# State-space groups with both halves of y behind the last panel, norm rows from picking products, and a 32-column low-rank gate

## The chip, the cores and the metric

One core of one Trainium2 chip runs the whole program. The metric is the device time of one execution in microseconds (us), median of the runs; lower is better. All arrays are float32 in HBM. The engines are TensorE (PE), VectorE (DVE), ScalarE (ACT), GpSimd (POOL) and SyncE (SP, which here only issues loads and stores). Code lines are written L1942 and the like.

## What is computed

The reference is two transformer-like blocks on x of 256 tokens by 1024 columns. The parts that the change touches:

```python
def ssd_scan(...):   # 8 groups of 4 heads, state 128, chunks of 128 tokens
    cum = jnp.cumsum(a_c, axis=1)
    decay = jnp.exp(jnp.where(causal, seg, -jnp.inf))
    y_intra = jnp.einsum('bgij,bghij,bjghp->bighp', cb, decay, x_c)
    y_inter = jnp.einsum('bign,bghpn->bighp', C_c, state) * jnp.exp(cum)[..., None]

def gated_group_rms_norm(y, z, w, groups):
    g = y * silu(z)
    gs = g.reshape(*g.shape[:-1], groups, -1)
    gs = gs * lax.rsqrt(jnp.mean(jnp.square(gs), axis=-1, keepdims=True) + EPS)
    return gs.reshape(g.shape) * w

log_a = jax.nn.log_sigmoid(gate_lr @ w_gate_up[l] + b_gate[l]) / GLA_GATE_TAU   # gate_lr: 16 columns of xn @ w_in
```

## The kernel before, in words

Activations lie transposed (columns on the 128 partitions, 256 tokens free). Every large weight streams from HBM as panels of 128x1024 (512 KB) into four slots of `raw`. For each slot ACT makes a rounded high part (`split_hi`, L491, 128x1024, type fp32r), DVE the remainder (`split_lo`, L980), and PE multiplies hi by hi, hi by lo and lo by hi (`panel`, L1665 to L1667: 24 products of 256 columns per panel). The counters `landed`, `hi_done`, `taken` and `used` pass a slot from SP to ACT, DVE and PE; SP loads the next panel into a slot when DVE has taken the last one out.

Between the convolution and the output products lies the state-space stage: eight groups g, one call of `ssd` each on PE (L1898 on), `ssd_act` on ACT (L682 on), `ssd_dve` on DVE (L1215 on) and `ssd_side` on POOL (L399 on), written out for g = 0 and 7 and in a loop over pairs for 1 to 6. In each group PE works on four panels of z and the gates, `zg_panel(0)` to `zg_panel(3)`, and puts the scan's small products between them:

- after panel 0: transposes of x and B, C times B (`cb_mm`), and two sums of segments (`seg_mm`) from `a_upto_hi` (made by POOL, L406) and `a_upto_lo` (made by ACT in `upto_low`, L680, eight 128x128 operations);
- after panel 1: the cumulative sum, spread over the partitions (L1930, L1931, `cum_mm`), whose exponential ACT writes to `c_in` (L691) and POOL multiplies by C (L420);
- after panel 2: the last group's norm sums (L1891), the new state (L1938, `st_mm`), which ACT copies to `state` (L699), and y of the first chunk (L1942);
- after panel 3: y of the second chunk (L1948 from `decay`, L1949 from `c_in` and `state`), then DVE adds it up (L1237).

ACT's order inside a group is: copy `b_tok`, two exponentials to `decay`, the exponential to `c_in`, `upto_low` for the next group, the high parts of slots 0 and 1, the copy of the mean and of `state`, three copies to `stg`, the high parts of slots 2 and 3, the panel sum out of PSUM (L504), the silu of z (L660), and, when DVE has multiplied y by it (L1246, the gate product), a square (L666). DVE interleaves four panels of the modulation matrix, which use the same four slots of `raw` (L990, L992): so slot 1 holds first a modulation panel, which DVE must take out in the next `ssd_dve`, and then the z panel that ACT converts.

After group 7 comes the gated norm. ACT issues five small loads from its own queue (L717), takes the mean and the root; DVE inverts it and writes `g_diag`, four tiles of diagonal matrices (L1267); PE multiplies each by ones (L1973, 128x512, two behind panel 2 of the gm stage and two behind panel 3), which spreads the rows over all partitions; DVE scales y by them (L1274), ACT and DVE split the result (`yb_hi` L728, `yb_lo` L1280), and the next stage's first product needs the first quarter of that. Each engine runs its instructions in the order written; nothing reorders them.

In the second block the low-rank gate is three products for each of 8 tiles (L2046 to L2048, 16 columns of weights), scaled by DVE to `glr_sb` (L1390) and multiplied by `wgu` (L2057).

## Time and profile before

| what | value |
|---|---|
| median of 3 runs | 927.41 us (926.66 to 929.55) |
| span of the profiled execution, first to last instruction | 925.2 us |
| own time of the profiled execution | not listed apart; its span and the some 2.2 us that lie between span and median |
| PE busy | 915.6 us (99%) |
| DVE busy | 706.2 us (76%) |
| ACT busy | 565.7 us (61%) |
| POOL busy | 100.7 us (11%) |
| PE on the chain that ended last | 96% |
| mean granted TensorE clock | 0.997 |

The span is the time from the first to the last instruction. The page lists busy time of each engine, then the span in 40 slices, the queues, the chain of work that ended last, and the costliest groups of instructions. The timeline has one line for each run of equal instructions: start, length, engine, line, tiles and, in brackets, how long the engine had sat idle before it and what ended that. Products overlap in PE, so the length of one (0.28 us for 256 columns) is more than its share; the distance from one start to the next is what it costs.

### The profile page before, as it was taken

The page shows a single profiled execution, that of the slowest core. Times are in us where ns is not written, and L with a number is a line of the kernel's source. Part 1 is how long each engine was busy: PE and PEld are TensorE (multiplying, and loading weights), DVE is VectorE, ACT ScalarE, POOL GpSimd, SP SyncE. Part 2 cuts the span into 40 slices and gives each one's busy share as a digit, 9 for nine tenths or more (in the row PEclk, how much of TensorE's full clock was granted, in tenths as well). Part 3 has the DMA queues.
Part 4 walks back from the last instruction along what each step waited for, and adds up shares of the span by engine and source line. Part 5 has one row for each costly group of instructions (what it writes and reads, how often), then busy time and mean ns, then how long its engine had stood idle before and what let it go on. Part 6 is the DMA issues. An engine that isn't in the chain of part 4 may idle for free.

```text
span 925.2 us, 17436 instructions
## 1 busy us (share of the span) xinstructions
PE 915.6 (99%) x6700; PEld 845.9 (91%) x6700; DVE 706.2 (76%) x952; ACT 565.7 (61%) x827; POOL 100.7 (11%) x88
## 2 busy tenths in 40 slices
PE   9999999999999999999999999999999999999997
PEld 6799999999999989989888888999879999999886
DVE  5957888889988968568777556689886798877663
ACT  4376655687877765456555345566665776666453
POOL 0000300024423300010000001403100200000001
PEclk9999999999999999999999999999999999999999
DMA  9954455577767756545655655535423365655661
GB/s 355 361 177 156 163 193 182 180 234 258 228 232 250 245 175 209 183 147 174 201 186 188 194 186 183 162 134 183 136 92 117 116 200 186 202 182 183 195 210 48
DMA packets 85564, 175.53 MB, mean 190 GB/s; under 512 B 5424, under 2 KB 46912, under 8 KB 85504
## 3 DMA queue, kind: packets, MB, share of 16 engines
q1 hardware_dynamic: 84384, 172.12, 56.2%
q10 hardware_dynamic: 752, 1.27, 0.4%
q0 software_dynamic: 368, 1.31, 0.4%
q8 instruction: 41, 0.67, 0.3%
q14 instruction: 19, 0.16, 0.1%
HBM read 173.63 MB, written 1.05 MB: 189 GB/s over the span
## 4 chain that ended last, share of the span: by engine, by line
PE 96%; DVE 2%; ACT 1%; POOL 0%; issue 0%; DVEq 0%; POOLq 0%
PE proj_ps L1665 18%; PE proj_ps L1682 17%; PE proj_ps L1666 17%; PE proj_ps L1667 17%; PE proj_ps L1685 9%; PE proj_ps L1754 1%; PE aux L1795 1%; PE proj_ps L1755 1%; PE proj_ps L1756 1%; PE aux L1786 1%; PE aux L2084 1%; PE aux L2111 1%; PE aux L1948 1%; DVE mod_acc L992 1%; PE aux L1810 1%; PE aux L1942 1%
## 5 line engine op out<-in xcount | busy, mean ns | idle before, releaser
L980 DVE TENSOR_TENSOR w_lo<-raw,w_hi 128x1024 fp32r<-128x1024 f32 x276 | 343.2, 1256 | 125.7 <-ACT w_hi L491 125.2
L491 ACT CAST w_hi<-raw 128x1024 fp32r<-128x1024 f32 x276 | 286.1, 1047 | 171.0 <-PE proj_ps L1667 70.4
L1665 PE MATMUL proj_ps<-act_pair,w_hi 128*128 128x256 f32 x1016 | 289.9, 285 | 0.0
L1667 PE MATMUL proj_ps<-act_pair,w_lo 128*128 128x256 f32 x1016 | 287.3, 283 | 0.0
L1666 PE MATMUL proj_ps<-act_pair,w_hi 128*128 128x256 f32 x1016 | 287.3, 283 | 0.0
L1665 PEld LDWEIGHTS proj_ps<-act_pair,w_hi 128*128 128x128 f32 x1016 | 194.7, 192 | 3.7 <-issue 1.5
L1666 PEld LDWEIGHTS proj_ps<-act_pair,w_hi 128*128 128x128 f32 x1016 | 194.8, 192 | 0.6
L1667 PEld LDWEIGHTS proj_ps<-act_pair,w_lo 128*128 128x128 f32 x1016 | 194.7, 192 | 0.0
L1682 PE MATMUL proj_ps<-ff_pair,w_hi 128*128 128x512 f32 x256 | 69.9, 394 | 0.0
L1682 PE MATMUL proj_ps<-act_pair,w_hi 128*128 128x512 f32 x248 | 67.7, 394 | 0.0
L439 POOL TENSOR_TENSOR tmp_b<-tmp_b 128x512 f32<-128x512 f32 x4 | 5.2, 1294 | 458.4 <-ACT tmp_b L514 458.4
L1682 PE MATMUL proj_ps<-glu_pair,w_hi 128*128 128x512 f32 x176 | 50.0, 395 | 0.0
L1682 PEld LDWEIGHTS proj_ps<-ff_pair,w_hi 128*128 128x128 f32 x256 | 43.7, 189 | 5.9
L1682 PEld LDWEIGHTS proj_ps<-act_pair,w_hi 128*128 128x128 f32 x248 | 42.4, 189 | 5.7
L992 DVE SCALAR_TENSOR_TENSOR mod_acc<-raw,silu_c,mod_acc 128x1024 f32<-128x1024 f32 x28 | 45.4, 1623 | 1.2 <-DMA raw<-in_panels 0.9
L1685 PEld LDWEIGHTS proj_ps<-ff_pair,w_lo 128*128 128x128 f32 x256 | 39.3, 189 | 5.5
L1685 PEld LDWEIGHTS proj_ps<-act_pair,w_lo 128*128 128x128 f32 x248 | 38.1, 189 | 5.3
L1685 PE MATMUL proj_ps<-ff_pair,w_lo 128*128 128x256 f32 x256 | 40.7, 281 | 0.0
L1685 PE MATMUL proj_ps<-act_pair,w_lo 128*128 128x256 f32 x248 | 39.5, 281 | 0.0
L1195 DVE SCALAR_TENSOR_TENSOR conv_acc<-proj_ps,cols,conv_acc 128x255 f32<-128x255 f32 (+2 forms) x96 | 38.7, 471 | 0.0
L1665 PE MATMUL proj_ps<-yb_hi,w_hi 128*128 128x256 f32 x128 | 36.3, 284 | 0.2 <-issue 0.2
L1667 PE MATMUL proj_ps<-yb_hi,w_lo 128*128 128x256 f32 x128 | 36.2, 283 | 0.0
(355 smaller groups left out, 1639.0 us busy)
## 6 DMA issues: line engine op xcount, KB each, us to landing
raw<-in_panels SPq DMA_DIRECT2D x308, 512.0 KB, 3.6
mod_first<-in_panels SPq DMA_DIRECT2D x16, 512.0 KB, 10.3
xres<-in_x_t SPq DMA_DIRECT2D x2, 512.0 KB, 5.5
wst<-in_ws_t POOLq DMA_DIRECT2D x1, 512.0 KB, 3.8
bs_sb<-in_bs_rows POOLq DMA_DIRECT2D x1, 512.0 KB, 4.6
level_sb<-in_levels ACTq DMA_DIRECT2D x1, 512.0 KB, 5.4
out_t<-tmp_a SPq DMA_DIRECT2D x1, 512.0 KB, 2.6
out_t<-tmp_a SPq DMA_DIRECT2D x1, 384.0 KB, 3.0
```

The lines of the kernel that those rows point to most:

```text
L491: nc.scalar.copy(w_hi[:, s, :], raw[:, s, :]).then_inc(hi_done, 1)
L980: tt(out=w_lo[:, s, :], in0=raw[:, s, :], in1=w_hi[:, s, :].bitcast(F32), op=ALU.subtract).then_inc(taken, 1)
L992: stt(out=mod_acc[:], in0=src, scalar=c_k, in1=mod_acc[:], op0=ALU.mult, op1=ALU.add).then_inc(done, 1)
L1195: ins = stt(out=out, in0=behind_nt, scalar=w(NT * c + nt, taps - 1 - back), in1=out, op0=ALU.mult, op1=ALU.add)
L1665: mm(dst, hi, xh, start=first and k == 0 and nt % 2 == 0, stop=False, skip_group_check=True)
L1666: mm(dst, hi, xl, start=False, stop=False, skip_group_check=True)
L1667: ins = mm(dst, lo, xh, start=False, stop=last and k == ks - 1, skip_group_check=True)
L1682: mm(bank, w_hi[:, s, n:n + P], flat(x_pair[:, k_at]), start=first and k == 0, stop=False, skip_group_check=True)
L1685: ins = mm(bank[:, T:2 * T], w_lo[:, s, n:n + P], x_hi[:, k_at], start=False, stop=False, skip_group_check=True)
L1754: mm(dst, xh, wh, start=first and k == 0, stop=False)
L1755: mm(dst, xh, wl, start=False, stop=False)
L1756: ins = mm(dst, xl, wh, start=False, stop=last and k == 1)
```

## The change

Four edits, which touch three stages.

1. **State-space group, PE.** `zg_panel(2)` goes ahead of the cumulative sum, so that this sum stands behind the third panel; y of the first chunk goes behind panel 3, directly ahead of y of the second chunk, and its wait asks for both decay tiles.
2. **State-space group, ACT.** The high part of slot 0 goes ahead of the exponential to `c_in`, the one of slot 1 behind it, and `upto_low` behind both, so that it stands directly ahead of the copies of the mean and of `state`.
3. **Gated norm.** `g_diag` is gone. DVE writes the inverse roots as a high part (columns 0 to 7) and a remainder (columns 32 to 39) of `g_part`; two products with a rounded identity turn them into rows (behind panel 1), ACT copies these to `g_rows`, and eight products with weights that pick one row and its remainder spread them over the partitions (behind panel 2). POOL makes `g_part`'s zeros, the identity and the picking weights behind its last group.
4. **Low-rank gate.** The high part and remainder of the weights stand side by side in 32 columns, so two products for each of 8 tiles take the place of three; rows 16 to 31 of the result are the remainder's, and `wgu` is loaded twice, into 32 partitions, so that the next product adds them. ACT's queue issues six loads in place of five.

```diff
@@ ssd_side, behind the last group
+            pool.wait_ge(S["cum_mm"], SSD_GROUPS + 1)
+            nc.gpsimd.memset(g_part[:].bitcast(F32), 0.0).then_inc(S["made_ok"], 1)
+            nc.gpsimd.tensor_tensor(out=ident_r[:], in0=ident, in1=ident, op=ALU.mult).then_inc(S["made_ok"], 1)
+            nc.gpsimd.tensor_tensor(out=pick_r[:], in0=ident[:, 0:SSD_GROUPS], in1=ident[:, 32:32 + SSD_GROUPS], op=ALU.add
+                                    ).then_inc(S["made_ok"], 1)
@@ ssd_act
+                split_hi(nxt, 0, landed_nxt)
                 act.wait_ge(S["cum_mm"], g + 2)
                 nc.scalar.activation(flat(c_in[:]), aux[:, 0], ACT.Exp).then_inc(S["ecum_ok"], 1)
+                split_hi(nxt, 1, landed_nxt)
                 if not last:
                     upto_low(g + 1)
-                split_hi(nxt, 0, landed_nxt)
-                split_hi(nxt, 1, landed_nxt)
                 act.wait_ge(S["st_mm"], g + 1)
                 if not first:
                     group_mean(g - 1)
@@ ACT, gated norm
-            for dst, src in ((rope_sb, rope_d), (level_sb, levels_d), (neg_sb, neg_d), (wgu, wgu_d), (wglr, wglr_d)):
-                act.dma_start(dst[:], src).then_inc(S["late_in"], 16)
+            for dst, src in ((rope_sb[:], rope_d), (level_sb[:], levels_d), (neg_sb[:], neg_d), (wgu[0:16, :], wgu_d), (wgu[16:32, :], wgu_d),
+                             (wglr[:], wglr_d)):
+                act.dma_start(dst, src).then_inc(S["late_in"], 16)
...
             split_hi(GROUP["ssm"], 0)
+            act.wait_ge(S["grow_mm"], 1)
+            nc.scalar.copy(g_rows[:], aux[:, 1, 0:T]).then_inc(S["copies_ok"], 1)
             split_hi(GROUP["ssm"], 1)
@@ DVE, gated norm
-            for q in range(4):
-                tt(out=g_diag[:, q], in0=spread(ident, 1, 4), in1=spread(g_stat[:, 1, 2 * q:2 * q + 2].rearrange("p g t -> p (g t)"), 2, P),
-                   op=ALU.mult).then_inc(S["gdiag_ok"], 1)
+            dve.wait_ge(S["made_ok"], 1)
+            roots = g_stat[:, 1].rearrange("p g t -> p t g")
+            g_hi, g_lo = g_part[:, :, 0:SSD_GROUPS], g_part[:, :, 32:32 + SSD_GROUPS]
+            step(nc.vector.tensor_copy(g_hi, roots))
+            tt(out=g_lo, in0=roots, in1=g_hi.bitcast(F32), op=ALU.subtract).then_inc(S["gpart_ok"], 1)
@@ ssd
                 zg_panel(1)
+                zg_panel(2)
                 pe.wait_ge(S["xdt_ok"], g + 1)
                 mm(aux[:, 0], ones_r[:], flat(a_upto_hi[:, 1]), start=True, stop=False)
                 mm(aux[:, 0], ones_r[:], flat(a_upto_lo[:, 1]), start=False, stop=True).then_inc(S["cum_mm"], 1)
-                zg_panel(2)
...
-                pe.wait_ge(S["m_ok"], g * 2 + 1)
+                zg_panel(3)
+                pe.wait_ge(S["m_ok"], g * 2 + 2)
                 for h in range(HPG):
                     mm(y(h, 0), xdt[:, 0, 64 * h:64 * h + 64], decay[:, 0, h], start=True, stop=True)
-                zg_panel(3)
-                pe.wait_ge(S["m_ok"], g * 2 + 2)
                 pe.wait_ge(S["state_ok"], g + 2)
                 pe.wait_ge(S["cin_ok"], g + 1)
@@ PE, gm stage
-                for q in ((), (), (0, 1), (2, 3))[s]:
-                    pe.wait_ge(S["gdiag_ok"], q + 1)
-
-                    pe.wait_ge(*((S["ecum_ok"], 9), (S["gs_ok"], 9), (S["y_ok"], 10), (S["mod_done"], 6))[q])
-                    mm(aux[:, q], ones[:], flat(g_diag[:, q]), start=True, stop=True).then_inc(S["grow_mm"], 1)
+                if s == 1:
+                    pe.wait_ge(S["made_ok"], 3)
+                    pe.wait_ge(S["gpart_ok"], 1)
+                    pe.wait_ge(S["gs_ok"], 9)
+                    for t in range(TT):
+                        ins = mm(aux[:, 1, t * P:t * P + P], g_part[:, t], ident_r[:], start=t == 0, stop=True, skip_group_check=True)
+                    ins.then_inc(S["grow_mm"], 1)
+                if s == 2:
+                    pe.wait_ge(S["copies_ok"], 2)
+                    for g in range(SSD_GROUPS):
...
+                        ins = mm(aux[:, q, (g % 2) * T:(g % 2) * T + T], spread(pick_r[:, g], 1, P), g_rows[:], start=g % 2 == 0,
+                                 stop=True, skip_group_check=True)
@@ PE, low-rank gate
-                dst = aux[0:16, 0, 0:T]
-                mm(dst, wglr_hi[:, k], pre2_hi[:, k], start=k == 0, stop=False)
-                mm(dst, wglr_hi[:, k], pre2_lo[:, k], start=False, stop=False)
-                ins = mm(dst, wglr_lo[:, k], pre2_hi[:, k], start=False, stop=k == KT - 1)
+                dst = aux[0:32, 0, 0:T]
+                mm(dst, flat(wglr_pair[:, k]), pre2_hi[:, k], start=k == 0, stop=False)
+                ins = mm(dst, flat(wglr_pair[:, k]), pre2_lo[:, k], start=False, stop=k == KT - 1)
```

The order of ACT's instructions in a state-space group, here group 0 from its exponentials to `decay` on; groups 1 to 6 repeat it. In these rows `w_hi<-raw` is the high part of a slot, slot 0 first. Before:

```order
L687 ACTIVATE decay<-aux 128x512 x2
L691 ACTIVATE c_in<-aux 128x512
L680 ACTIVATE a_upto_lo<-square,a_lo 128x128 x8
L491 CAST w_hi<-raw 128x1024 x2
L699 COPY state<-aux 128x256
L641 COPY stg<-xbc 128x512
```

With the change (the lines are those of the changed kernel):

```order
L695 ACTIVATE decay<-aux 128x512 x2
L499 CAST w_hi<-raw 128x1024
L700 ACTIVATE c_in<-aux 128x512
L499 CAST w_hi<-raw 128x1024
L688 ACTIVATE a_upto_lo<-square,a_lo 128x128 x8
L707 COPY state<-aux 128x256
L649 COPY stg<-xbc 128x512
```

The eight operations on `a_upto_lo` stood ahead of both conversions and now stand between the second one and the copy of `state`.

ACT at the gated norm, from the last of its small loads to the first copy of `yb_hi`. Before:

```order
L717 DMA wglr<-in_wglr 128x128
L671 COPY g_stat<-aux 128x2
L721 ACT_TABLE_LOAD
L721 ACTIVATE g_stat<-g_stat,eps 128x16
L722 ACT_TABLE_LOAD
L722 ACTIVATE zg<-zg 128x2048
L491 CAST w_hi<-raw 128x1024 x2
L725 ACTIVATE zg<-zg 128x2048
L728 CAST yb_hi<-xbc 128x1024
```

With the change:

```order
L726 DMA wgu<-in_wgu 16x256 x2
L726 DMA wglr<-in_wglr 128x128
L679 COPY g_stat<-aux 128x2
L730 ACT_TABLE_LOAD
L730 ACTIVATE g_stat<-g_stat,eps 128x16
L731 ACT_TABLE_LOAD
L731 ACTIVATE zg<-zg 128x2048
L499 CAST w_hi<-raw 128x1024
L734 CAST g_rows<-aux 128x256
L499 CAST w_hi<-raw 128x1024
L736 ACTIVATE zg<-zg 128x2048
L739 CAST yb_hi<-xbc 128x1024
```

One load more is issued ahead of the mean, and the copy to `g_rows`, with its wait for PE's two turning products, stands between the two conversions.

## Rows read from the trace of the kernel before

**Rows 1.** The page, part 1 (busy us, share of the span, instructions)

```profile
PE 915.6 (99%) x6700; PEld 845.9 (91%) x6700; DVE 706.2 (76%) x952; ACT 565.7 (61%) x827; POOL 100.7 (11%) x88
```

**Rows 2.** Waits of PE: who waited for whom, us in total, times, longest us

```profile
PE aux L1795 <- DVE zero L1091: 2.1, 1, 2.1
```

**Rows 3.** Timeline of PE, group 3: start us, us, instruction

```profile
250.57 0.39 PE L1665 MATMUL proj_ps<-act_pair,w_hi 128*128 128x256 f32 x1
...
253.63 0.45 PE L1948 MATMUL aux<-decay,xdt 128*64 128x128 f32 x4
```

**Rows 4.** Timeline of ACT, group 3

```profile
246.35 0.60 ACT L691 ACTIVATE c_in<-aux 128x512 f32<-128x512 f32 x1 [0.83 <-PE aux L1931]
246.84 2.44 ACT L680 ACTIVATE a_upto_lo<-square,a_lo 128x128 fp32r<-128x128 f32 x8
...
250.89 1.05 ACT L491 CAST w_hi<-raw 128x1024 fp32r<-128x1024 f32 x1 [0.68 <-DMA raw<-in_panels]
...
251.90 0.38 ACT L699 COPY state<-aux 128x256 f32<-128x256 f32 x1
...
254.95 1.05 ACT L491 CAST w_hi<-raw 128x1024 fp32r<-128x1024 f32 x1 [0.60 <-DMA raw<-in_panels]
```

**Rows 5.** Timeline of DVE, its gate product of groups 2 and 3

```profile
241.50 0.69 DVE L1246 TENSOR_TENSOR xbc<-xbc,zg  x1 [0.17 <-ACT zg L660]
...
259.06 0.69 DVE L1246 TENSOR_TENSOR xbc<-xbc,zg  x1 [0.94 <-ACT zg L660]
```

**Rows 6.** Timeline of SP: the load of slot 1, and all loads (the page, part 6)

```profile
246.53 0.34 SPq L297 DMA_DIRECT2D raw<-in_panels  x1
...
raw<-in_panels SPq DMA_DIRECT2D x308, 512.0 KB, 3.6
```

**Rows 7.** Timeline of PE, the same instruction two groups apart

```profile
241.80 0.48 PE L1926 MATMUL aux<-a_upto_hi,after_r 128*128 128x512 f32 x1
...
277.12 0.48 PE L1926 MATMUL aux<-a_upto_hi,after_r 128*128 128x512 f32 x1
```

**Rows 8.** Timeline of PE, norm rows and what follows

```profile
336.79 1.88 PE L1973 MATMUL aux<-g_diag,ones 128*128 128x512 f32 x4
...
343.45 0.36 PE L1665 MATMUL proj_ps<-yb_hi,w_hi 128*128 128x256 f32 x1 [0.18 <-issue]
```

**Rows 9.** Timeline of ACT at the gated norm

```profile
330.72 0.45 ACTq L717 DMA_DIRECT2D wgu<-in_wgu  x1
...
332.04 0.16 ACT L671 COPY g_stat<-aux 128x2 f32<-128x2 f32 x1 [2.06 <-PE aux L1891]
...
341.04 1.05 ACT L728 CAST yb_hi<-xbc 128x1024 fp32r<-128x1024 f32 x1 [0.29 <-DVE xbc L1274]
```

**Rows 10.** Timeline of DVE at the gated norm

```profile
333.93 0.25 DVE L1265 RECIPROCAL g_stat<-g_stat 128x16 f32<-128x16 f32 x1 [3.54 <-ACT g_stat L721]
334.21 2.50 DVE L1267 TENSOR_TENSOR g_diag<-square,g_stat 128x512 f32<-128x512 f32 x4
...
342.12 1.22 DVE L1280 TENSOR_TENSOR yb_lo<-xbc,yb_hi 128x1024 fp32r<-128x1024 f32 x1 [1.11 <-ACT yb_hi L728]
```

**Rows 11.** Timeline of ACT: a copy of 128x256 from PSUM in another stage

```profile
605.65 0.37 ACT L526 COPY rr_sb<-aux 128x256 f32<-128x256 f32 x1 [1.24 <-PE aux L1779]
```

**Rows 12.** Timeline of PE, DVE and POOL: low-rank gate product, first level

```profile
609.76 0.28 PE L2046 MATMUL aux<-pre_hi,wglr_hi 128*16 128x256 f32 x1
...
612.49 0.28 PE L1665 MATMUL proj_ps<-act_pair,w_hi 128*128 128x256 f32 x1
...
613.92 0.41 DVE L1390 TENSOR_TENSOR glr_sb<-aux,rr_sb 16x256 f32<-16x256 f32 x1
...
635.72 0.87 POOL L473 TENSOR_TENSOR gx<-gqk,gd 128x256 f32<-128x256 f32 x1
...
636.97 1.16 PE L2084 MATMUL aux<-gx 64*128 64x128 f32 x16
```

**Rows 13.** Windows of 2 us: busy (x), then PEclk (granted clock), DMA share, GB/s

```profile
22.00:24.00 2.00, 2.00 (x3) 0.82 (x3) 1.79 (x6) 0.91 (x2) 0.72 (x1) 0.50 1.05 400
```

More of the change, by code:

```diff
@@ L139, in two_blocks @@
         yb_lo = at("yb_lo", 88, [16, T], F32R)
-        g_diag = at("g_diag", 152, [4, 4, P])
+        g_part = at("g_part", 160, [TT, P], F32R)
+        g_rows = at("g_rows", 161, [T], F32R)
+        pick_r = at("pick_r", 162, [SSD_GROUPS], F32R)
+        ident_r = at("ident_r", 162.5, [P], F32R)
         g_sq = at("g_sq", 202.5, [2, T])
@@ L250, in two_blocks @@
             "an engine's own steps": "dve_step pool_step",
-            "memsets and first conversions": "ready c_ready narrow_hi_ok narrow_ok ws_masked",
+            "memsets and first conversions": "ready c_ready narrow_hi_ok narrow_ok copies_ok ws_masked made_ok",
             "modulation": "mod_acc_ok mod_mm mod_done",
@@ L258, in two_blocks @@
                    "btok_ok decay_ok ecum_ok state_ok",
[L259 removed]
+            "gated group norm": "silu_z sig_ok g_ok g2_ok gsq_ok gs_mm gs_ok grt_ok gpart_ok grow_mm yb_f yb_h yb_ok",
             "mixers' sum": "mix_f mix_h mix_ok",
             "first MLP": "sq_ok ffhi_ok ff_ok",
[L262 removed]
+            "GLA": "glr_mm glr_ok gate_mm gx_abs gx_exp gx_u gx_ln gx_inv lev_d lev_e lev_x lev_mm lev_ok "
                    "og_mm og_sq og_ms og_rt og_diag og_row gla_f gla_h gla_ok",
@@ L634, in _ @@
             nc.scalar.copy(after_r[:], after)
-            nc.scalar.copy(ones_r[:], ones[:]).then_inc(S["sums_ok"], 1)
+            nc.scalar.copy(ones_r[:], ones[:]).then_inc(S["copies_ok"], 1)
             def group_tiles(g, par):
@@ L779, in _ @@
             scale2 = lambda k: small[:, 88 + k:89 + k]
-            act.wait_ge(S["late_in"], 80)
-            nc.scalar.copy(wglr_hi[:], wglr[:]).then_inc(S["narrow_hi_ok"], 1)
+            act.wait_ge(S["late_in"], 96)
+            nc.scalar.copy(wglr_hi, wglr[:]).then_inc(S["narrow_hi_ok"], 1)
             unscaled_hi(range(4), pre2_hi, RES_FF2, scale2)
```

33 lines of the change are left out of this document (18 added, 15 removed).

## The prediction

> **What bounds the kernel now.** I read the page's busy times first: PE is busy 99% of the span [rows 1]. Then the waits of PE: the longest is 2.1 us ahead of its very first product [rows 2], and no wait of PE in the state-space stage is in the list at all. So PE's own instructions set the end, and the change can act in two ways: take products away from PE, or make PE wait where it does not now. The first is counted from distances between starts; for the second the timelines of ACT, DVE and SP beside PE must be read, since the change reorders ACT and leaves PE's slack to be found out. The chip's differences of under about 0.3% (2.8 us) can't be told from no change here.
>
> **Low-rank gate (edit 4).** The 24 products run from 609.76 to 612.49, 0.114 us each [rows 12]. Eight go: 0.9 us less for PE. The next reader of the result, DVE's scaling, ends at 614.33 on a chain of its own and PE would come about then, so that wait stays near zero. But the first level product that needs POOL starts at 636.97, and POOL's operand was complete at 636.59 [rows 12]: 0.4 us of slack. If that chain doesn't move with PE, only 0.4 us of the 0.9 stays. Bounds 0 and -0.9; I take **-0.4**, since the slack row is the nearest thing to a limit.
>
> **Gated norm (edit 3).** PE's side: two pairs of diagonal products, 1.88 us each pair [rows 8], so 3.8 us go; ten short products at the 0.114 us of [rows 12] come, 1.1 us. PE alone would gain 2.6 us. But the stage behind starts at 343.45, just after DVE's first `yb_lo` ends at 342.12 + 1.22 = 343.34 [rows 8, 10]: that chain sets the start, not PE. Its links are ACT's. It was late already: the mean was copied 2.06 us after ACT fell idle of computing, because ACT's queue was issuing loads [rows 9]. One more load costs the 0.45 us of its neighbour [rows 9]. The copy to `g_rows` costs the 0.37 us of an equal copy [rows 11]. Against both stands ACT's idle 0.29 us ahead of `yb_hi` [rows 9]. Sum 0.45 + 0.37 - 0.29 = 0.53. DVE's side loses four `g_diag` products, 2.50 us, for two tiny ones (the reciprocal of 128x16 is the nearest, 0.25 each) [rows 10]; that moves only work that waits for ACT afterwards. PE also waits twice inside: its turning products need `g_part` at about 334.18 + 0.45 + 0.5 = 335.1, while panel 1 ends some 2.9 us (24 products at 0.12) ahead of the 336.79 of [rows 8], at 333.9: 1.2 us. It would catch up none of this by the saving, as the chain ends it anyway. So the 2.6 us are not gained, and the net is **+0.6**; bounds -2.6 (chain hidden after all) and +1.5 (the 0.29 us not there, ACT later). POOL's three setup operations stand behind its last group's work; POOL is busy 11% [rows 1], and I count nothing. If that cover fails, each costs PE at most what a POOL operation here takes, 0.9 us [rows 12].
>
> **State-space groups, PE (edit 1).** The same products in another place. Between panel 3's first product and y's second chunk lie 253.63 - 250.57 = 3.06 us [rows 3]. What a change of neighbour does to a start is about 0.1 to 0.2 us either way (3.06 against 24 times 0.12 = 2.88), so eight groups are bounded by -1.6 and +1.6; I take 0. The exponential to `c_in` moves a panel later, from 246.35 [rows 4] to about 249.2; POOL's product behind it is then done by about 251.9, if it takes at most twice the 0.87 us of its other operations [rows 12] and a start; y needs it from 253.6 on. Covered by panel 3. What is queued behind ACT's longer wait is the conversion of slot 1, whose panel lands only at 250.8 anyway.
>
> **State-space groups, ACT (edit 2): the term that decides.** In group 3 the conversion of slot 1 starts at 250.89, ended by the landing of its panel, and `state` is copied from 251.90 to 252.28 [rows 4]. PE needs `state` for y at 253.63 [rows 3]. Slack: 1.35 us. Before, the eight `a_upto_lo` operations, 2.34 us from start to next start (246.84 to 249.18), ran while ACT had nothing to convert [rows 4]. Now they run behind the slot 1 conversion, and nothing but the landing decides when that is. So `state` is ready at 252.28 + 2.34 = 254.62: PE waits **1.0 us**. That is the first turn.
>
> It doesn't stop there, because ACT, DVE and SP form a ring. From the slot 1 conversion ACT goes on to the `stg` copies, slots 2 and 3, the panel sum and the silu; then DVE's gate product, its modulation panels 0 and 1; then SP's load into slot 1, and the next conversion. ACT's part, 250.89 to 259.06, is 8.17 us, of which 0.60 was a wait for slot 3's landing [rows 4, 5]; with the 2.34 us inside and the 0.60 swallowed it is 9.91. DVE's and SP's part, 241.50 to 250.89, is 9.39 [rows 4, 5]. The ring becomes 19.3 us. PE's group takes (277.12 - 241.80) / 2 = 17.66 us [rows 7]. So the ring would be 1.6 us longer than PE's group and becomes the bound: first turn 1.0, then five more groups up to group 6 (group 7 makes no next `a_upto_lo`), 1.0 + 5 x 1.64 = 9.2 us. That is the upper bound. Downwards: slot 1's load takes 250.89 - 246.53 = 4.36 us, behind its neighbours, while the median of all loads is 3.6 [rows 6]. With loads further apart it would tend to that, 0.76 less a turn: 1.0 + 5 x 0.88 = 5.4 us. The lowest end is the first turn alone, 1.0, if the ring has slack that I don't see. I take **6.0**, near the lower of the two rings, since a late ACT spaces SP's loads by itself. At the end ACT is late against PE by part of a turn, and the gated norm's chain starts from there: bounds 0 and +1.0, I take +0.3.
>
> The Trainium skill, page "DMA: Bandwidth & Descriptors", section "Anatomy of one DMA — SWDGE (gpsimd) path", gives a DMA (one issued from GpSimd; these come from SP) some 2.0 us fixed and its bytes at 436 GB/s, an estimate of 3.2 us for 512 KB. By that the ring would be 18.1 us, and this term 1.0 + 5 x 0.5 = 3.5 instead of 6.0, the time 931.4. The trace disagrees for this slot, with 4.36 us.
>
> **Sum**, against the profiled execution: 925.2 - 0.4 + 0.6 + 0 + 6.0 + 0.3 = 931.7 us of span. Around the span lie 2.2 us (927.41 - 925.2, the profiled execution taken as a median one), so **933.9 us**, +0.7%.
>
> **Rivals.**
>
> *A, the ring stays open: no change.* The first turn's 1.0 us is paid once, then PE's own delay gives ACT its slack back. For it: ACT was idle 0.68 and 0.60 us ahead of two of its conversions [rows 4], so some of what is inserted fills idle time, and the ring is read from one group alone. Against it: 19.3 against 17.66 us. Time: 927.4 + 1.0 + 0.6 - 0.4 = 928.6.
>
> *B, PE's saved products count: faster.* The place is the copy of `state` in each group: if it lies 1.0 us earlier than I work out (slot 1 landing at 249.8 instead of 250.8), PE does not wait, and if the gated norm's chain is also shorter, since DVE loses 2 us of `g_diag`, PE gains its 2.6. Time: 927.4 - 2.6 - 0.9 - 0.8 (half of the bound of edit 1) = 923.1. It decides from a landing under 3.4 us after issue on. For it: PE is at 99%, and every product removed was on its path. Against it: ACT's idle row names the DMA.
>
> *C, the clock falls as well.* The granted clock was 0.50 from 22 to 24 us, in a stretch with thin products, and PE was busy all of it [rows 13]: such a drop costs 1 us for each 2 us that it lasts. Waits of 1 to 2 us in each group could bring it about. Six drops: 933.9 + 6 = 940. Against it: nothing shows that a wait of 1 us does this. The Trainium skill, page "TensorE: Matmul & The Clock Gate", section "A second HAM failure mode: psum-queue depth-cycling", tells of a kernel whose short idle times between groups of products made the clock go up and down; by it this rival would be the forecast. No row here shows it.
>
> *D, the change doesn't do what it says.* The conversions could run ahead of landings they wait for in another count. The order of ACT's instructions shows the move, so I give this nothing of its own.
>
> **Chances and range.** My forecast (the ring closes, 930.5 to 938) 0.66; A 0.17; B 0.12; C 0.05. Slower by over 0.3% (above 930.2) takes the forecast and C, less a little of the forecast's low end, plus the top of A: 0.70. Within 0.3%: 0.18. Faster: 0.12. The range reaches down into A and up over the ring's likely sizes: 926.5 to 938. The forecast's own range is 930.5 to 938.
>
> **What would show it.** Right: PE lists waits for ACT's `state` copy, under 0.5 us in some groups and 1 to 2.5 in others, together 5 to 9; the distance of two groups grows from 35.3 to 37 or more; ACT's conversion of slot 1 is still ended by a DMA and `a_upto_lo` follows it; PE waits about 1.2 us for `g_part`; the stage behind the norm starts 6 us or more later. Wrong: no wait of PE in the groups and the distance still 35.3, or the first product on `yb_hi` earlier than 343.4. If the clock is under 0.99 in the groups, C holds.

## The result, and the profile after

The changed kernel is slower: 939.39 us (median of 4 runs, 937.4 to 942.8) against 927.95 for the kernel before, a ratio of 1.0127 with a 95% interval of 1.0106 to 1.0148. Run again beside other kernels it took 939.65 (median of 6 runs, 934.0 to 947.8). The direction, the place and the largest term of the forecast were right. The time lies 5.5 us above the forecast and 1.4 us above its range.

The profiled execution (the one of 937.4 us, the fastest of the four) spans 935.7 us, 10.5 more than before. Its page, part 1:

```profile
PE 917.6 (98%) x6694; PEld 850.8 (91%) x6694; DVE 699.3 (75%) x950; ACT 565.0 (60%) x828; POOL 102.3 (11%) x91
```

PE has six products fewer than in [rows 1] and is busy 2.0 us longer. Idle time alone could not do that: some products take longer. The waits of PE (us in total, times, longest us) now begin with a line that [rows 2] did not have:

```profile
PE aux L1960 <- ACT state L707: 6.8, 5, 2.4
PE aux L1808 <- DVE zero L1102: 2.1, 1, 2.1
PE proj_ps L1678 <- issue: 1.0, 1, 1.0
```

The timeline of ACT in group 3 answers to [rows 4]:

```profile
250.73 1.05 ACT L499 CAST w_hi<-raw 128x1024 fp32r<-128x1024 f32 x1 [1.61 <-DMA raw<-in_panels]
251.69 0.59 ACT L700 ACTIVATE c_in<-aux 128x512 f32<-128x512 f32 x1
253.70 1.05 ACT L499 CAST w_hi<-raw 128x1024 fp32r<-128x1024 f32 x1 [1.42 <-DMA raw<-in_panels]
254.65 2.44 ACT L688 ACTIVATE a_upto_lo<-square,a_lo 128x128 fp32r<-128x128 f32 x8
...
257.04 0.36 ACT L707 COPY state<-aux 128x256 f32<-128x256 f32 x1
```

And PE at the same place, with [rows 3] to compare:

```profile
255.10 0.66 PE L1956 MATMUL aux<-decay,xdt 128*64 128x128 f32 x8
257.46 0.45 PE L1960 MATMUL aux<-decay,xdt 128*64 128x128 f32 x4 [1.70 <-ACT state L707]
```

`upto_low` stands behind a conversion whose start waited for a landing, and the copy of `state` behind `upto_low`; PE sits idle for 1.70 us. Over all groups the waits are 1.17, 1.30, 0.22, 1.70, 0, 2.41, 0, 0: uneven, as when PE runs up to a slower chain. Two groups take 36.7 to 40.5 us instead of the 35.32 of [rows 7].

The rest is the clock. Windows of the changed kernel (busy, then PEclk, DMA share, GB/s):

```profile
294.00:295.00 1.00, 0.05 (x2) 0.06 (x3) 1.00 (x1) 1.00 (x5) 0.68 (x1) 1.00 0.05 8
296.00:302.00 6.00, 6.00 (x30) 5.80 (x28) 3.84 (x5) 4.86 (x7) 0.00 (x0) 0.50 0.69 221
303.00:304.00 1.00, 1.00 (x12) 1.00 (x12) 0.00 (x0) 0.00 (x0) 0.31 (x1) 1.00 0.59 225
340.00:343.00 3.00, 3.00 (x16) 3.00 (x17) 0.00 (x0) 1.20 (x2) 0.00 (x0) 0.52 0.98 367
927.00:930.00 3.00, 3.00 (x11) 1.97 (x11) 0.17 (x1) 0.66 (x2) 0.00 (x0) 0.54 0.00 0
```

PE was idle up to 294.95, its longest wait; from 295.8 to 302.6 the granted clock stands at half (1.2 instead of 2.4 GHz), and PE does 30 products in 6 us (some of them longer ones) where it does 12 in one us just behind. What this costs is read from the same stretch of products with and without the drop, from y's second chunk to the next group's segment sums, in groups 5 and 3:

```profile
294.95 0.45 PE L1960 MATMUL aux<-decay,xdt 128*64 128x128 f32 x4 [2.41 <-ACT state L707]
...
304.69 0.47 PE L1939 MATMUL aux<-a_upto_hi,after_r 128*128 128x512 f32 x1
```

```profile
264.15 0.48 PE L1939 MATMUL aux<-a_upto_hi,after_r 128*128 128x512 f32 x1
```

It takes 9.74 us with the drop and 264.15 - 257.46 = 6.69 without: 3.0 us. The clock also stands at half at 340, behind a wait of 0.65 us for the last square, and at 927, at the end of the program.

Where the 10.5 us lie is told by how far the same product is behind its place in the trace of before:

| product | before | changed | behind by |
|---|---|---|---|
| last run of products of y, group 7 | 324.99 | 333.53 | 8.54 |
| first product on `yb_hi` | 343.45 | 353.19 | 9.74 |
| first gate product | 609.76 | 619.48 | 9.72 |
| second level product | 636.97 | 646.15 | 9.18 |
| end of the span | 925.2 | 935.7 | 10.5 |

- The groups cost 8.5 us: 6.8 of waits for `state` and 3.0 of clock, less 1.3 for the PE order's shorter groups and other small differences.
- The norm stage costs 1.2 us, none of it the clock's. Between the copy of the panel mean and the first product on `yb_hi` lie 11.4 us in both kernels (332.04 to 343.45 and 341.78 to 353.19). The mean is copied 1.2 us later behind the last y: 0.8 because ACT's last square comes later (5.16 us behind that y instead of 4.36), and 0.4 because ACT's queue then issues six loads. The drop at 340 falls into time that PE has to spare before `yb_hi`, where it is idle for 1.04 us even so.
- The gate gives back 0.5 us. Its own products are 0.9 us shorter, as the lines below show, but the level products behind it wait for POOL: 26.67 us lie between the first gate product and the second level product, where [rows 12] have 27.21.
- The drop at 927 costs 1.3 us. It stands in code that the change does not touch, some 600 us behind the last wait in the groups; the second profile of the changed kernel (`after_again`, below) has none there while PE works, so nothing shows that the change brought it about.

```profile
619.48 0.28 PE L2070 MATMUL aux<-pre_hi,wglr_pair 128*32 128x256 f32 x1
...
621.30 0.28 PE L1678 MATMUL proj_ps<-act_pair,w_hi 128*128 128x256 f32 x1
...
646.15 1.16 PE L2107 MATMUL aux<-gx 64*128 64x128 f32 x16
```

That is 1.82 us between the first two starts, where [rows 12] have 2.73.

### The profile page after: what moved, and what is told of

It is laid out like the page before. It is cut to its first block, busy times and chain, and to the rows that moved or that the text cites. A ratio compares the mean times of both kernels' runs of the same rounds, so it can differ in the third digit from the quotient of the medians.

```text
span 935.7 us, 17426 instructions
## 1 busy us (share of the span) xinstructions
PE 917.6 (98%) x6694; PEld 850.8 (91%) x6694; DVE 699.3 (75%) x950; ACT 565.0 (60%) x828; POOL 102.3 (11%) x91
## 4 chain that ended last, share of the span: by engine, by line
PE 79%; DVE 6%; ACT 6%; DMA 4%; issue 3%; POOL 1%; ACTq 0%; DVEq 0%; SPq 0%; POOLq 0%
PE proj_ps L1695 17%; PE proj_ps L1678 14%; PE proj_ps L1679 13%; PE proj_ps L1680 13%; PE proj_ps L1698 9%; DMA raw<-in_panels 3%; DVE mod_acc L1003 2%; PE proj_ps L1767 1%; DVE w_lo L991 1%; PE proj_ps L1768 1%; PE proj_ps L1769 1%; ACT a_upto_lo L688 1%; ACT w_hi L499 1%; PE aux L1799 1%; DMA mod_first<-in_panels 1%
## 5 line engine op out<-in xcount | busy, mean ns | idle before, releaser
L991 DVE TENSOR_TENSOR w_lo<-raw,w_hi 128x1024 fp32r<-128x1024 f32 x276 | 348.9, 1276 | 126.4 <-ACT w_hi L499 125.6
L1003 DVE SCALAR_TENSOR_TENSOR mod_acc<-raw,silu_c,mod_acc 128x1024 f32<-128x1024 f32 x28 | 39.2, 1399 | 1.0 <-DMA raw<-in_panels 0.7
```

The costliest lines, as they stand in the source:

```text
L991: tt(out=w_lo[:, s, :], in0=raw[:, s, :], in1=w_hi[:, s, :].bitcast(F32), op=ALU.subtract).then_inc(taken, 1)
L1003: stt(out=mod_acc[:], in0=src, scalar=c_k, in1=mod_acc[:], op0=ALU.mult, op1=ALU.add).then_inc(done, 1)
```

## Experiments

Three theories. **R**: what stands on ACT between the cumulative sum and `state`, or the ring of ACT, DVE and loads, makes PE wait. **C**: the granted clock falls behind such waits and costs extra. **P**: PE's own length, or its new order, counts. Later ones are split off: L (a local chain on ACT ahead of the `state` copy), D (DVE's product into `decay` has no slack left) and N (ACT's queue of small loads sets the norm's chain). All ratios are to the kernel before, run on the same chip beside them (926.98 to 927.51 us).

### The two orders apart

`low_first`, against the changed kernel:

```diff
                 nc.scalar.activation(flat(c_in[:]), aux[:, 0], ACT.Exp).then_inc(S["ecum_ok"], 1)
-                split_hi(nxt, 1, landed_nxt)
                 if not last:
                     upto_low(g + 1)
+                split_hi(nxt, 1, landed_nxt)
```

> The changed kernel with one line moved on ACT: the conversion of slot 1 of the next panel stands behind the eight upto_low instead of ahead of them; all else as in the change. Theory R (the waits come from ACT's order: the eight upto_low, 19.5 us a turn against PE's 17.6): the waits of PE before y's second chunk (6.8 us in all in the changed kernel) are gone, two groups take 35.2 us again, and the time falls by 6.8 us at least, to about 932. Theory C (the drops of the granted clock at 295.8 and 340.1 come behind those waits, and cost about 4 us): they are gone too, and the time is near 926, a little below the kernel before, as the gate's 0.9 us and the PE order's 0.7 us are left. Theory P (the waits come from PE's own new order, which needs m and xdt earlier or later): the waits and the 939 stay.

Measured: 931.02 us, 1.0044 (1.0027 to 1.0062). One line on ACT takes back some 8 of the 11.4 us. The waits fell from 6.8 to 2.7 us and no clock drop is left in the groups. But 926 was not reached; something else costs.

`act_order_only` is the kernel before with edit 2 alone, `pe_order_only` the kernel before with edit 1 alone (the diff of the change, those lines only).

> The kernel before with the ACT order alone (slots 0 and 1 of the next panel converted ahead of the eight upto_low). Theory R: PE waits for the second product's state copy as in the changed kernel, 5 to 8 us over eight groups, and the time is 933 to 936. With theory C the clock falls behind the largest of these waits, 2 to 4 us more: 936 to 939. Theory P: no wait, 927.4.

Measured: 936.34 us, 1.0101 (1.0064 to 1.0138); 5.5 us of waits at that place, and a clock of 0.5 for 3.4 us behind one of 1.3 us. As R and C say. (The profile names no releaser for these waits; the place is y's second chunk, which waits for `state`.)

> The kernel before with the PE order alone (y's first chunk behind the group's last panel, the spread cumulative sum behind the third). Theory R: no new wait; the products saved (0.09 us a group in the changed kernel) give 0.7 us: 926.7. Theory P: PE waits before y or the spread sum, and the time is 932 to 939.

Measured: 933.35 us, 1.0063 (1.0042 to 1.0084). A miss for what I had written under R; the time is in the range written under P, a new order that makes PE wait. PE waits for `state` in seven groups:

```profile
PE aux L1947 <- ACT state L699: 6.5, 7, 1.3
```

each 0.87 to 0.89 us but the first, with no growth: not a ring, but a local chain. ACT and PE in group 3 of that kernel:

```profile
251.90 0.60 ACT L691 ACTIVATE c_in<-aux 128x512 f32<-128x512 f32 x1 [2.33 <-PE aux L1932]
252.39 2.44 ACT L680 ACTIVATE a_upto_lo<-square,a_lo 128x128 fp32r<-128x128 f32 x8
254.73 1.98 ACT L491 CAST w_hi<-raw 128x1024 fp32r<-128x1024 f32 x2
...
256.67 0.37 ACT L699 COPY state<-aux 128x256 f32<-128x256 f32 x1
```

```profile
257.09 0.45 PE L1947 MATMUL aux<-decay,xdt 128*64 128x128 f32 x4 [0.87 <-ACT state L699]
```

The cumulative sum comes a panel later, ACT stands still for 2.33 us waiting for it, and the 5.1 us of work from `c_in` to `state` don't fit before y.

Neither order is harmless: one costs 6.4 us alone and the other 9.4, and the whole change 11.4 to 12.1. So the two do not add up. That each uses up the same slack, the 1.35 us that I had found between `state` and y, would explain it; no run shows it apart.

### Which half of the PE order

`cum_move_only` moves the cumulative sum alone (L1930, L1931 behind `zg_panel(2)`), `y_move_only` y's first chunk alone (L1942 behind `zg_panel(3)`), both in the kernel before.

> The kernel before with the spread cumulative sum alone moved behind the third panel. Theory L: the whole of what the PE order costs is here. The sum comes 2.9 us later, of which 1.35 us were slack and 0.68 us idle: PE waits 0.9 us in each of seven groups, 933 to 934. If it is the move of y's first chunk instead: 927.

> The kernel before with y's first chunk alone moved behind the last panel. Theory L: nothing waits, since y's second chunk starts where it did, and the products between two kinds saved give 0.09 us a group: 926.3. If the first chunk's move costs PE's order its slack: 930 or more.

Measured: 934.10 us, 1.0069 (1.005 to 1.0088), and 928.56 us, 1.0005 (0.9984 to 1.0026). The sum's move carries the loss, with 0.74 to 0.75 us of wait in each of six groups after a first one of 1.14. The other move can't be told from no change. Its waits are of another kind:

```profile
PE aux L1943 <- DVE decay L1232: 2.5, 3, 1.2
```

The first chunk used to need only the first half of DVE's product into `decay`; behind the last panel PE asks for both halves 0.66 us (the length of the first chunk) sooner than before.

### Other orders on ACT and DVE

`state_first` and `state_then_slot`, against the changed kernel (the second has `split_hi(nxt, 1, ...)` ahead of `upto_low`, otherwise the same):

```diff
                 nc.scalar.activation(flat(c_in[:]), aux[:, 0], ACT.Exp).then_inc(S["ecum_ok"], 1)
-                split_hi(nxt, 1, landed_nxt)
-                if not last:
-                    upto_low(g + 1)
                 act.wait_ge(S["st_mm"], g + 1)
                 if not first:
                     group_mean(g - 1)
                 nc.scalar.copy(state[:], aux[:, 1, 0:T]).then_inc(S["state_ok"], 1)
+                if not last:
+                    upto_low(g + 1)
+                split_hi(nxt, 1, landed_nxt)
```

> The changed kernel with ACT's copies of the panel mean and of state right behind the exponential to c_in, then the eight upto_low, then the conversion of slot 1. Theory L (a local chain: what stands on ACT between the spread cumulative sum and the state copy makes PE wait, 0.9 us a group in the PE order alone, whose waits did not grow from group to group): no wait of PE ahead of y's second chunk, two groups take 35.2 us, no drop of the granted clock in the groups, the time is 925 to 926.5. Theory R (the ring of ACT, DVE and SP is longer than PE's group whatever its order): the wait turns up elsewhere, at a panel or at the transposes, 4 to 6 us in all, time 930 to 934.

> As the one before, but the conversion of slot 1 ahead of the eight upto_low, as in the change. Theory L: as before it, 925 to 926.5. Theory R: the ring has the 2.4 us of upto_low inside again (between the conversions of slot 1 and slot 3), so that PE waits at the panels of the next group, 5 us or more, and the time is 932 or more.

Measured: 932.52 us, 1.0051 (1.0033 to 1.007), and 934.65 us, 1.0083 (1.0062 to 1.0104). Theory L falls, R holds: no line for `state` is left, but two groups still take 35.7 to 36.8 and 36.7 to 37.9 us. The wait turned up at DVE's product into `decay` (2.6 us in both), at the modulation columns (0.9 and 3.7 us) and, in group 7, at POOL's product behind `c_in` (0.9 us in both).

`state_first_dve` is `state_first` with DVE's fourth modulation panel of a group moved behind both products into `decay`; `y_late_dve` has that edit, y's first chunk late, and otherwise both old orders (with the norm and gate edits).

```diff
+                mod_panel_of(2)
                 for c in range(2):
-                    mod_panel_of(2 + c)
                     dve.wait_ge(S["decay_ok"], g * 2 + (c + 1))
...
                        op=ALU.mult).then_inc(S["m_ok"], 1)
+                mod_panel_of(3)
```

> The kernel with the state copy first (on record above: 932.5 us; PE waited 2.6 us for DVE's product into decay, 0.9 for POOL's product behind c_in, 0.9 for a modulation column) with DVE's fourth modulation panel behind the second product into decay. Theory D: the 2.6 us go, the others may stay: 929 to 931. If the ring of loads behind it sets the pace whatever the order: 932 to 934, the wait at another place.

> The changed kernel with ACT's old order and the cumulative sum back behind the second panel, so that of the two orders only y's first chunk behind the last panel is left; and on DVE the fourth modulation panel of a group moved behind the second product into decay. Theory D (with y's first chunk late PE needs that second product 0.7 us earlier, and DVE, 0.8 us ahead of it in group 3 before, has no slack left): now DVE has 2 us more, PE does not wait, two groups take 35.15 us, and the time is 926.0 - 0.7 = 925.3. If the waits stay (DVE's lateness comes from the gate product before, not from its own order): 927 to 929.

Measured: 932.52 us, 1.0058 (1.0039 to 1.0078), and 935.72 us, 1.0085 (1.0065 to 1.0104). The first is where `state_first` was. The second is the clearest miss of the study: 7 us slower than `y_move_only`, which is y's late chunk without the DVE edit (and without the norm and gate edits, which change nothing that can be told, as shown below). The waits for `decay` are gone, as theory D had it, and others, larger, stand in their place:

```profile
PE aux L1940 <- DVE modc L1027: 6.0, 3, 2.7
PE aux L1944 <- DVE xdt L1232: 2.5, 4, 0.8
```

Why is seen on ACT, at the conversion of slot 3 in group 3:

```profile
261.38 1.05 ACT L499 CAST w_hi<-raw 128x1024 fp32r<-128x1024 f32 x1 [2.35 <-DMA raw<-in_panels]
```

The modulation panel sits in slot 3 of `raw` until DVE has taken it; taken later, it lets the next load start later, and the 0.60 us of wait for that landing in [rows 4] has become 2.35. ACT's panel sum and silu come later by that, then DVE's gate product, then everything DVE does for the next group. This is the ring, closed through a load.

### The clock: filling PE's idle time

`fill`, against the changed kernel, puts six products a group between y's first chunk and the wait for `state`; `fill_more` has twelve of them. They write to a part of PSUM that the next panel overwrites. `after_again` is the changed kernel once more.

```diff
+                for n in range(0 if last else 6):
+                    mm(proj_ps[:, par, 0:256], after_r[:], x_hi[:, n], start=True, stop=True)
                 pe.wait_ge(S["state_ok"], g + 2)
```

> The changed kernel with six products more on PE (128x256, 0.12 us each, 0.7 us in all) in groups 0 to 6, ahead of its wait for the state copy; their result is overwritten, so nothing of the output changes. Theory R (another chain sets the pace and PE only waits for it): the waits shrink by what is filled, the places of y stay, and the products cost nothing, except in the groups without a wait (0.7 us each, three of seven): 937 to 941. If the clock's drops came from the idle time as such, they go with it, and the time is 1 to 3 us lower than that: 935 to 938. If PE's own length counts (theory P): 939.4 + 7 x 0.7 = 944.

> The changed kernel with twelve filler products (1.4 us) in groups 0 to 6 ahead of PE's wait for the state copy. Theory R and C (the pace is another chain's, and PE's idle time lets the granted clock drop): waits under 1.5 us in all, no or one drop in the groups, and a time of 936 to 940, though PE has 9.8 us more of products than the changed kernel. Theory P (PE's own length counts in full): 939.4 + 9.8 = 949.

> The changed kernel once more, beside the kernels with filler products, on one chip. 937 to 942, mean granted clock 0.983 to 0.992, as in its first four runs; a profile with 5 to 8 us of waits for the state copy, and at least one stretch at a clock of 0.5 between 200 and 350 us.

Measured:

| kernel | added to PE (7 groups) | median us | ratio (95%) | mean granted clock over its runs | waits for `state`, profiled run |
|---|---|---|---|---|---|
| changed kernel, again | none | 939.65 | 1.0133 (1.0089 to 1.0177) | 0.989 | 6.7 us |
| fill | 5.4 us | 935.87 | 1.0095 (1.0070 to 1.0121) | 0.993 | 2.4 us |
| fill_more | 10.9 us | 937.44 | 1.0107 (1.0079 to 1.0136) | 0.997 | none |

(The added time is 84 products at the 0.13 us that each takes, by the two-group distance below; for the 42 of `fill` it is an estimate from that.) With 10.9 us of useless work PE is no slower: P as PE's own length, by which `fill_more` would take 949 us, is out, and another chain sets the pace. That `fill` is faster is likely and not beyond doubt, since its interval and those of the two sets of the changed kernel (1.0106 to 1.0148 and 1.0089 to 1.0177) overlap a little. It is what R and C together give: the work fits into time in which PE would have waited, so it costs little, and PE falls idle less, so the clock stays. The clock in the groups says the same: the two profiles of the changed kernel have one drop and three there, `fill` and `fill_more` none. The unfilled kernel, run beside `fill_more`:

```profile
259.66 0.45 PE L1960 MATMUL aux<-decay,xdt 128*64 128x128 f32 x4 [2.28 <-ACT state L707]
```

```profile
262.00:269.00 7.00, 7.00 (x42) 7.00 (x42) 3.32 (x5) 4.08 (x5) 0.73 (x1) 0.63 0.72 215
```

and, with twelve fillers, its clock over the whole span:

```profile
core 0: 935.3 us, clock 1.000
```

The 1.000 owes something to luck: this execution also lacks the drop near the program's start that the other profiles have, in a stretch that no kernel here changes. With twelve the groups are evenly 38.25 us a pair, the 35.15 of PE's own products (the 36.91 of `pe_order_only` less its two waits of 0.88) and two fillings of 1.55: there PE itself sets the pace again. Six are nearer to what the other chain leaves free.

How much is clock in all? In the profiled execution it is 4.3 of the 10.5 us, 3.0 in the groups and 1.3 at the end. Over all runs only an upper figure can be had. The span times the mean granted clock is what a run would take at the full clock throughout, roughly. Its median is 922.3 us over 83 runs of the kernel before, and 926.4 and 927.8 us over the two sets of the changed kernel. So of the 11.4 to 12.1 us of loss 4 to 5.5 us remain at the full clock, and at most some 7 us are clock; at most, because a drop in time that PE has to spare, as at 340, is counted here and costs nothing.

The Trainium skill, page "TensorE: Matmul & The Clock Gate", section "A second HAM failure mode: psum-queue depth-cycling", describes this kind of case: short idle times between groups of products that make the clock go down and up. The traces agree, with 6.8 us at half clock behind a wait of 2.4 us. They also show that idle time is not enough by itself: `pe_order_only` waited 0.88 us in every group and kept a mean clock of 0.996, as the kernel before, and `y_late_dve` waited 2.73 us ahead of the segment sums of a group, with a full panel right behind, and had no drop there. And it is not needed everywhere: in `y_move_only` the clock fell from 332.2 to 335.8, in the norm stage, though PE had not waited as much as 0.2 us in the 40 us before; what stood there were sixteen products of one column each and a full panel:

```profile
329.99 0.95 PE L1786 MATMUL aux<-ones,mod_acc 128*128 128x1 f32 x8
331.08 1.05 PE L1891 MATMUL aux<-avg_g,g_sq 128*128 128x1 f32 x8
332.00 0.36 PE L1665 MATMUL proj_ps<-ya_hi,w_hi 128*128 128x256 f32 x1
```

### Norm and gate edits

`norm_rows_only` is the kernel before with edit 3 alone; `norm_gate` has edits 3 and 4 with both old orders.

> The kernel before with the norm edit alone (transpose by four products, copy on ACT, eight picking products). In the changed kernel this stretch lost 1.2 us, with a clock of 0.5 for 3.4 us at 340. If that drop belongs to the waits of the groups ahead of it: no drop here, the first product on yb_hi 0.5 us sooner to 0.3 us later than before, the time 927 to 928. If the drop belongs to the norm's own short wait and short products: the clock falls at 331 to 335 here too, and the time is 928.5 to 929.5.

> The changed kernel with both engines' orders in the state-space groups put back (edits 1 and 2 undone), norm and gate edits kept. No wait of PE in the groups, two groups take 35.33 us, no drop of the granted clock between 26 and 920 us. The norm edit alone gave 0.34 us in the trace, the gate's eight products 0.9 us: span 925.2 - 0.3 - 0.9 = 924.0, time about 926.0, faster than both kernels by a little. If the norm or the gate edit had a share in the changed kernel's loss: 928 or more.

Measured: 927.26 us, 0.9998 (0.9978 to 1.0019), and 928.07 us, 1.0006 (0.9988 to 1.0023). Neither can be told from the kernel before. The traces say more than the times do. The first product on `yb_hi`, at 343.45 before [rows 8], starts at 343.12 with the norm edit, and at 344.23 with the gate edit on top, though that edit touches nothing of the norm but ACT's list of loads. From the copy of the mean to that product it is 11.4 us in all three, so the norm edit takes nothing off the chain and adds nothing to it; the 0.33 us come from ACT's queue, whose last load took 0.72 us to issue in the trace of before and 0.44 in `norm_rows_only`. The timeline of ACT in `norm_gate`, to be read beside [rows 9]:

```profile
330.67 1.52 ACTq L726 DMA_DIRECT2D wgu<-in_wgu  x2
332.22 0.48 ACTq L726 DMA_DIRECT2D wglr<-in_wglr  x1
332.83 0.16 ACT L679 COPY g_stat<-aux 128x2 f32<-128x2 f32 x1 [2.89 <-issue]
```

The two loads of `wgu`, of 16x256 each, take 1.52 us to issue, where the one took 0.45, and the panel mean is copied at 332.83, against 332.04 before and 331.71 with the norm edit alone. So the 0.5 us that the gate edit saves behind 610 us, and more, are lost at 331 us, on a queue that nobody would look at for a low-rank gate.

So the loads were moved behind the conversions of `yb` (`late_only`: in the kernel before, with its five loads; `norm_gate_late`: with edits 3 and 4, whose diff against the changed kernel is shown without its old orders):

```diff
-            for dst, src in ((rope_sb[:], rope_d), (level_sb[:], levels_d), (neg_sb[:], neg_d), (wgu[0:16, :], wgu_d), (wgu[16:32, :], wgu_d),
-                             (wglr[:], wglr_d)):
-                act.dma_start(dst, src).then_inc(S["late_in"], 16)
             group_mean(7)
...
+            for dst, src in ((rope_sb[:], rope_d), (level_sb[:], levels_d), (neg_sb[:], neg_d), (wgu[0:16, :], wgu_d), (wgu[16:32, :], wgu_d),
+                             (wglr[:], wglr_d)):
+                act.dma_start(dst, src).then_inc(S["late_in"], 16)
             for j in range(2):
```

> The kernel before with ACT's five loads for the level stage moved from ahead of the last panel mean to behind the conversions of yb. Theory N (ACT's queue, busy with issuing loads for 2.1 us, sets the gated norm's chain, and so the start of the stage behind): ACT copies the mean 1.7 us sooner, and the first product on yb_hi comes up to 1.0 us sooner; PE's own products (two diagonal pairs, 3.8 us) then bound it. 926.0 to 927.0. If PE's products set it: no change, 927.3.

> Norm and gate edits with both old orders, and the six loads moved behind the conversions of yb. With the loads ahead (on record: norm and gate edits) the sixth load cost the norm's chain 1.1 us and gave the gate's 0.9 back. Theory N: the mean is copied 2.5 us sooner, PE has 2.6 us less of products, and the first product on yb_hi comes 1.5 to 2.5 us sooner than in that kernel: span 923.0 to 924.0, time 924.8 to 925.8, the fastest of all. If ACT's two sigmoids and conversions set it anyway: 926.5 or more.

Measured: 927.44 us, 0.999 (0.9972 to 1.0008), and 927.02 us, 0.999 (0.9973 to 1.0007). The chain of `norm_gate_late` is shorter:

```profile
331.14 0.16 ACT L679 COPY g_stat<-aux 128x2 f32<-128x2 f32 x1 [1.21 <-PE aux L1904]
```

```profile
342.54 0.35 PE L1678 MATMUL proj_ps<-yb_hi,w_hi 128*128 128x256 f32 x1 [1.05 <-issue]
```

1.7 us sooner than in `norm_gate`. The profiled span is 923.7 us, the shortest of all kernels here; by its interval the time is not shown to be faster than before. With the loads moved in the kernel before alone, the stretch from the last y to the first product on `yb_hi` is 0.8 us shorter (325.90 to 343.59, against 324.99 to 343.45). In that trace one more wait of PE takes it back, 1.0 us for DVE's product into `decay` in group 1, ahead of any edited place. Why the median shows no gain either, no run here tells.

## Why the prediction was wrong in size

- **What bounds, and where it would show: right.** PE waits for ACT's `state` copy, five waits with 6.8 us in all; the forecast was 6.0, and "together 5 to 9". The two-group distance is over 36.7. The value lies between the two rings that I worked out (5.4 and 9.2).
- **The step that failed: the sum counted the clock at nothing.** It stood as rival C with 0.05, "against it: nothing shows that a wait of 1 us does this". The term is 4.3 us in the profiled execution (3.0 behind the wait of 2.41 us, 1.3 at the end of the program) and at most some 7 us over the runs. C's sign, a clock under 0.99 in the groups, came true: it is 0.98 from 190 to 334 us, in the row below this item. C's figure, 940, is close to what was measured (939.4), in part by luck: it had six drops of 2 us, one a group, and there were one of 6.8 us in one profile and three of 3.4 to 6.8 us in the other. The chance given was too small, and the range should have reached to C, since its condition (waits of 1 to 2 us, from my own sum) was met by the forecast itself: C was no rival to the ring but its consequence, though not a sure one.

```profile
190.00:334.00 144.00, 137.19 (x1142) 130.43 (x1140) 117.21 (x118) 106.47 (x191) 50.07 (x40) 0.98 0.70 226
```

- **The rest of the distance is small.** The forecast has 931.7 us of span, the profile 935.7. The waits are 0.8 us more than the 6.0, the clock 4.3, the norm stage 1.2 instead of 0.9; the groups are otherwise 1.3 shorter than the 0 of edit 1, and the gate gives 0.1 more. The other 2.0 us of the median are that the profiled execution was the fastest of four; the two slowest, of 940.60 and 942.78 us, had a lower mean clock (0.987 and 0.983 against its 0.990).
- **Edit 1 "takes 0": wrong as a statement on the edit.** I worked out the late cumulative sum with ACT's new order only. Alone it costs 6.4 us (933.35 against 926.98). On top of edit 2 it can't be told from nothing (1.0101 with edit 2 alone, 1.0127 with all four, and the intervals overlap). PE's own products are 0.09 us a group shorter in `pe_order_only`, inside the bounds of 1.6.
- **Edit 2: right in size (6.8 us of waits against 6.0), with too simple a cause.** With `upto_low` back ahead of slot 1 (`low_first`) the kernel is still 4 us slower than before, since a part of edit 1's loss then shows. The 1.35 us of slack that I read was the slack of one chain. DVE's product into `decay` had another, which I did not read at all. In the trace of before, group 3:

```profile
251.55 1.25 DVE L1232 TENSOR_TENSOR decay<-decay,cbm 128x512 f32<-128x512 f32 x1 [0.19 <-DVE mod_acc L992]
```

  It ends at 252.80, 0.83 us ahead of y at 253.63 [rows 3], and the late first chunk takes 0.66 of that.
- **Edit 3 with the sixth load: +0.6 forecast, and +0.3 for a late ACT.** In the profile it is +1.2. The copy to `g_rows` and the 0.29 us came to nothing together, as the 11.4 us from the mean to `yb_hi` did not change. The load was put at the 0.45 of its neighbour; it moved the mean by 0.4 us in the changed kernel and by 1.1 in `norm_gate` against `norm_rows_only`. A late ACT cost 0.8. The wait for the turning products was forecast as 1.2 us; it is 1.46 in `norm_gate` and 1.06 in the second profile of the changed kernel, and none in the first, where the clock drop at 340 to 343.6 takes its place.
- **Edit 4: -0.4 forecast, -0.5 measured: right, and by the mechanism named.** PE's products end 0.9 us sooner and POOL's chain does not follow in full, so that part of it stays. The slack was read at the second level product; the first stands at 632.81, with 0.59 us of slack.
- **The load's time.** The rule of the Trainium skill, page "DMA: Bandwidth & Descriptors", section "Anatomy of one DMA — SWDGE (gpsimd) path", would have made the ring term 3.5 us. The measured 6.8 stands against it; the median landing of all panel loads even went from 3.6 us [rows 6] to 3.9.

What stays open: which share of the spread from run to run comes from the start of the program, where the clock stands at half for 3.4 us in most profiles, for 6.8 in one, for 13.7 in two, and once not at all. No kernel here changes anything in that stretch. What decides whether a drop follows a wait is open too: filling the waits also gave PE more work, and no run changes the one without the other. And a combination of ACT and DVE orders that lets the late cumulative sum pay was not found; four were tried besides the change's own and the old one.

## What to carry to other kernels

In a loop where four engines pass the same few buffers round, read the slack of every engine's hand-over in a group before one is used up: taking the wait at one place away showed the next one at once (in `state_first`, `state_then_slot`, `state_first_dve` and `y_late_dve`), and a step moved later on one engine came back as a late load. When a sum forecasts idle time of PE in every turn, the price of a lower clock belongs in the sum and not among the rivals; here it was 4.3 us in the profile, beside 6.8 us of waits. A cheap test is to fill the idle time with throw-away products: if the time does not grow, another chain sets the pace, and if it falls, the clock was part of the loss. And before a drop of the clock or a shorter product is counted, ask whether PE is on the path there: the drop at 340 and the norm's saved products both moved nothing. Compare the distance between two fixed products in both traces, not the lengths.

## What was not expected of the hardware

- Adding 42 products of 256 columns in places where PE waited made the program no slower and probably faster (939.65 to 935.87 us, ratios 1.0133 and 1.0095); with 84 it took 937.44 us, though they fill 10.9 us.
- In the second profile of the changed kernel the clock fell 0.6 to 2.0 us behind the end of waits of 1.37, 2.28 and 1.64 us, for 3.4, 6.8 and 3.4 us, but not behind one of 1.39 us just before. In the first profile it fell behind 2.41 us and, at 340, behind 0.65 us, but not behind 1.70. In `act_order_only` it fell behind 1.28 us after three waits of 1.17 to 1.39 us without a drop. `y_late_dve` had none behind 2.73 us, and `y_move_only` had one with no wait of 0.2 us near it. So no length of a single wait tells whether a drop follows.
- A load of 16x256 from ACT's own queue took 0.45 us to issue once, but two in a row took 1.13 (changed kernel) and 1.52 us (`norm_gate`), with ACT computing nothing meanwhile. The load behind it took 0.72 us in the trace of before and 0.44 to 0.48 in those of `norm_rows_only`, `norm_gate` and the changed kernel.
